# Two-layer encoder with expert-choice routing: top-k states in four quarters, and router weights that carry the norm's weights

## What is computed

```python
h = rms_norm(x, norm_ffn[i])
affinity = softmax(h @ w_router, axis=-1)          # 16 experts
gate, idx = lax.top_k(affinity.T, cap)             # cap = 2 * T / 16
xe = tokens[idx]
hid = silu(xe @ w_gate) * (xe @ w_up)
ye = (hid @ w_down) * gate[..., None]
out = zeros.at[idx].add(ye)
```

## Time and profile before

| | before |
|---|---|
| median of 3 runs | 1827.52 us |
| the profiled execution, its own time | 1825.45 us |
| span of the profile | 1823.6 us |
| PE busy | 1757.9 us (96%) |
| DVE busy | 1330.9 us (73%) |
| ACT busy | 1131.5 us (62%) |
| POOL busy | 234.7 us (13%) |
| mean DMA rate | 266 GB/s |

### The profile page before, as it was taken

One profiled execution on the slowest core, in us unless ns is written; L12 is line 12 of the kernel. 1 busy time (PEld: TensorE's weight loads), 2 busy tenths in 40 slices (PEclk: granted clock), 3 DMA queues, 4 the chain that ended last, 5 costly groups with the idle time before them and its releaser, 6 DMA issues.

```text
span 1823.6 us, 24589 instructions
## 1 busy us (share of the span) xinstructions
PE 1757.9 (96%) x10322; PEld 1386.7 (76%) x10322; DVE 1330.9 (73%) x1008; ACT 1131.5 (62%) x1185; POOL 234.7 (13%) x118
## 2 busy tenths in 40 slices
PE   6999989999999999999999999999999999999997
PEld 6888889977766776776779987997677677667765
DVE  4735455688888888888855556557888888888885
ACT  4343452457777777777743557335777777777774
POOL 0100000000110010010011100000112211311311
PEclk9999999999999999999999999999999999999998
DMA  4411123389999999999964012338999999999994
GB/s 161 102 45 56 43 69 107 156 321 396 396 375 388 393 379 382 394 382 377 396 200 104 21 39 55 106 118 326 376 394 383 378 390 393 377 383 390 375 393 141
DMA packets 155841, 486.00 MB, mean 266 GB/s; under 512 B 12199, under 2 KB 46119, under 8 KB 155687
## 3 DMA queue, kind: packets, MB, share of 16 engines
q1 hardware_dynamic: 148308, 459.26, 66.9%
q0 software_dynamic: 7424, 25.17, 5.9%
HBM read 454.26 MB, written 30.13 MB: 266 GB/s over the span
## 4 chain that ended last, share of the span: by engine, by line
PE 91%; DVE 3%; ACT 3%; issue 1%; DMA 1%; POOL 0%; POOLq 0%; SPq 0%; DVEq 0%; ACTq 0%
PE ps L1817 19%; PE ps L1819 19%; PE ps L1818 19%; PE ps L1515 5%; PE ps L1517 4%; PE ps L1516 4%; PE ps L1595 3%; PE ps L1469 3%; PE ps L1707 2%; PE ps L1709 2%; PE ps L1708 2%; PE ps L1567 2%; PE ps L1788 1%; PE ps L1584 1%; PE ps L1781 1%
## 5 line engine op out<-in xcount | busy, mean ns | idle before, releaser
L1320 DVE TENSOR_TENSOR w_lo<-ring,w_hi 128x2048 fp32r<-128x2048 f32 x384 | 876.7, 2291 | 144.5 <-ACT w_hi L1024 144.3
L1024 ACT ACTIVATE w_hi<-ring 128x2048 fp32r<-128x2048 f32 x384 | 735.6, 1917 | 275.0 <-PE ps L1819 268.2
L1817 PE MATMUL ps<-w_hi,xe_hi 128*96 128x512 f32 x1016 | 403.5, 397 | 0.0
L1819 PE MATMUL ps<-w_hi,xe_lo 128*96 128x512 f32 x1016 | 399.3, 393 | 0.0
L1818 PE MATMUL ps<-w_lo,xe_hi 128*96 128x512 f32 x1016 | 398.2, 392 | 0.0
L1819 PEld LDWEIGHTS ps<-w_hi,xe_lo 128*96 128x96 f32 x1016 | 163.9, 161 | 71.4
L1817 PEld LDWEIGHTS ps<-w_hi,xe_hi 128*96 128x96 f32 x1016 | 163.8, 161 | 69.8 <-DVE xe_lo L1419 5.9
L1818 PEld LDWEIGHTS ps<-w_lo,xe_hi 128*96 128x96 f32 x1016 | 164.3, 162 | 64.6
L1817 PE MATMUL ps<-w_hi,hid_hi 128*96 128x512 f32 x512 | 201.6, 394 | 0.0
L1819 PE MATMUL ps<-w_hi,hid_lo 128*96 128x512 f32 x512 | 201.1, 393 | 0.0
L1818 PE MATMUL ps<-w_lo,hid_hi 128*96 128x512 f32 x512 | 200.3, 391 | 0.0
(11 more groups left out here) (190 smaller groups left out, 2243.3 us busy)
## 6 DMA issues: line engine op xcount, KB each, us to landing
ring<-in_moe_w_gate SPq DMA_DIRECT2D x128, 1024.0 KB, 7.5
ring<-in_moe_w_up SPq DMA_DIRECT2D x128, 1024.0 KB, 8.9
ring<-in_moe_w_down SPq DMA_DIRECT2D x128, 1024.0 KB, 9.2
wbuf<-in_a_w_in SPq DMA_DIRECT2D x9, 1024.0 KB, 5.6
ffn_rows<-hrow SPq DMA_DIRECT2D x12, 512.0 KB, 2.7
wbuf<-in_b_w_in SPq DMA_DIRECT2D x5, 1024.0 KB, 7.8
unit_rows<-row SPq DMA_DIRECT2D x36, 132.0 KB, 1.8
bias<-bias_rows SPq DMA_DIRECT2D x4, 768.0 KB, 10.1
```

Of the source, the lines that this page charges most:

```text
L1024: nc.scalar.activation(w_hi[:, n % SPLIT], ring[:, n % RAW], ACT.Copy).then_inc(hi_split, 1)
L1320: nc.vector.tensor_tensor(w_lo[:, n % SPLIT], ring[:, n % RAW], w_hi[:, n % SPLIT].bitcast(F32), ALU.subtract).then_inc(lo_split, 1)
L1817: nc.tensor.matmul(out, hi[:, k, :], w_hi[:, n % SPLIT, i, cols], start=(k == 0), stop=False)
L1819: ins = nc.tensor.matmul(out, lo[:, k, :], w_hi[:, n % SPLIT, i, cols], start=False, stop=(k == KM - 1))
```

## The change

The norm's weights are multiplied into the router's weights (gain_router), so PE turns x itself for the router. hrow is made in one DVE instruction with both factors, one tile later (norm_row), and ACT scales it no more. The top-k states lie in four quarters of 32 partitions: each replacement (strike) reads one quarter and writes the next, so four successive states stand side by side, and one index search serves four rounds (find). The prompt's rows are rows 16 to 31 of the quarters; they join at round 6, and the rounds 8 and 9 are 256 columns wide. The results are packed by products with a constant mask (place) and brought to the layout of take by matmuls with a constant (expert). On SP, three pieces go ahead of the last row store, two behind it, and the sixth waits for the first gather. The idle products before the picks are 16 instead of 28. The two constants are loaded at the start, before the third weight chunk, and DVE waits for them with the other constants.

```diff
 C = CS + CP
-RAW, SPLIT = 6, 4
+RAW, SPLIT, FRONT = 6, 4, 3
 KP = 2
...
         buckets[BUCKETS, start + i] = MASKED
-    return {"c_buckets": buckets, "c_ident": np.eye(P, dtype=np.float32)}
+    row = np.arange(P)
+    quarter = np.zeros((P, 6, 8), np.float32)
+    for at, q in enumerate((0, 1, 2, 3, 2, 3)):
+        quarter[row // 32 == q, at, :] = 1.0
+    expert = (row[:, None] % 32 == np.arange(2 * NE)[None, :]).astype(np.float32)
+    return {"c_buckets": buckets, "c_ident": np.eye(P, dtype=np.float32), "c_quarter": quarter, "c_expert": expert}
...
 router = sb("router", [P, KM, NE])
+gain_col = sb("gain_col", [P, KM])
+quarter = sb("quarter", [P, 6, 8])
+expert = sb("expert", [P, 2 * NE])
+aff_p = sb("aff_p", [P, PT_, 2 * NE])
...
     hrow = sb("hrow", [P, NT, DM], scope=mo)
-    am = sb("am", [48, DEC_SEQ], scope=mo)
-    topi = sb("topi", [48, CS], U32, scope=mo)
-    pk_i = sb("pk_i", [48, P], scope=mo)
-    pk_g = sb("pk_g", [48, P], scope=mo)
+    am = sb("am", [P, DEC_SEQ], scope=mo)
+    top_v = sb("top_v", [P, 3, 8], scope=mo)
+    top_i = sb("top_i", [P, 3, 8], U32, scope=mo)
+    pick_i = sb("pick_i", [P, C], scope=mo)
+    pick_v = sb("pick_v", [P, C], scope=mo)
     xg = sb("xg", [C, 2, DM], scope=mo)
...
         sp.dma_start(router[:], d["moe_router"][layer].rearrange("(k p) e -> p k e", p=P)).then_inc(route_in, 16)
+        sp.dma_start(gain_col[:], bass.AP(d["norm_ffn"].tensor, layer * DM, [[1, P], [P, KM]]),
+                     allow_slow_non_contiguous=True).then_inc(route_in, 16)
...
             t = ORDER[i]
-            sp.wait_ge(row_scaled, NT * layer + i + 1)
+            sp.wait_ge(h_ready, NT * (2 * layer + 1) + i + 1)
             sp.dma_start(h_d[t * P:(t + 1) * P, :], hrow[:, t, :]).then_inc(h_out[i % 2], 16)
...
         sp.wait_ge(out_done, NT * (layer + 1))
-        for n in range(layer * LAYER_PIECES, layer * LAYER_PIECES + RAW):
+        first_piece = layer * LAYER_PIECES
+        for n in range(first_piece, first_piece + FRONT):
             load_piece(n)
         store_rows(NT - 1)
+        for n in range(first_piece + FRONT, first_piece + RAW - 1):
+            load_piece(n)
         sp.wait_ge(xg_in[0], 16 * (layer * NE // 2 + 1))
-        for n in range(layer * LAYER_PIECES + RAW, (layer + 1) * LAYER_PIECES):
+        for n in range(first_piece + RAW - 1, first_piece + LAYER_PIECES):
             load_piece(n)
-            if n == layer * LAYER_PIECES + RAW + 1:
+            if n == first_piece + RAW + 1:
                 store_sums(NT - 1)
...
-        def scale_rows(i):
-            t = ORDER[i]
-            act.wait_ge(rstd_ready, rstd_count(2 * layer + 1, i))
-            nc.scalar.activation(hrow[:, t, :], hrow[:, t, :], ACT.Copy, scale=rstd[:, t:t + 1]).then_inc(row_scaled, 1)
         def exp_route(part):
...
             act.wait_ge(rlog_ready, 2 * layer + part + 1)
+            act.wait_ge(rstd_ready, rstd_count(2 * layer + 1, (NT - PT_ if part == 0 else NT) - 1))
             for t in range(STREAM[part].start, STREAM[part].stop):
...
                 take_rows(i - 1)
-                scale_rows(i - 1)
             if i == NT - PT_:
...
         take_rows(NT - 1)
-        scale_rows(NT - 1)
         exp_route(1)
...
     nc.vector.memset(minus_half[:], -0.5)
+    nc.vector.memset(aff_p[:], 0.0)
     nc.vector.memset(rb, 1.0).then_inc(rb_set, 1)
...
-        def gain_row(i):
+        def norm_row(i):
             t = ORDER[i]
             dve.wait_ge(attn_added, NT * layer + i + 1)
-            nc.vector.tensor_tensor(hrow[:, t, :], x[:, t, :], gain[:], ALU.mult).then_inc(h_ready, 1)
+            dve.wait_ge(rstd_ready, rstd_count(2 * layer + 1, i))
+            nc.vector.scalar_tensor_tensor(hrow[:, t, :], x[:, t, :], rstd[:, t:t + 1], gain[:],
+                                           ALU.mult, ALU.mult).then_inc(h_ready, 1)
+        def gain_router():
+            dve.wait_ge(route_in, 32 * (layer + 1))
+            nc.vector.tensor_tensor(router[:], router[:], gain_col[:].unsqueeze(2).to_broadcast([P, KM, NE]),
+                                    ALU.mult).then_inc(router_ready, 1)
...
             step(nc.vector.reciprocal(lrec[:, ts], lsum[:, ts]), route_step)
-            nc.vector.tensor_tensor(aff[:, ts, :], lexp[:, ts, :],
+            nc.vector.tensor_tensor(aff[:, ts, :] if part == 0 else aff_p[:, :, NE:2 * NE], lexp[:, ts, :],
                                     lrec[:, ts].unsqueeze(2).to_broadcast([P, ts.stop - ts.start, NE]),
...
             else:
-                step(nc.vector.tensor_copy(am[32:32 + NE, 0:SEQ], ps[0:NE, 4, 0:SEQ]), route_step)
-        def top_round(rows, r, last):
-            cols, w = slice(8 * r, 8 * r + 8), DEC_SEQ if rows.start == 0 else SEQ
-            best = pk_g[rows, cols]
-            step(nc.vector.max(best, am[rows, 0:w]), route_step)
-            step(nc.vector.max_index(topi[rows, cols], best, am[rows, 0:w]), route_step)
-            if not last:
-                step(nc.vector.match_replace(am[rows, 0:w], best, am[rows, 0:w], -1.0), route_step)
-        SAMPLE, BOTH, PROMPT = slice(0, NE), slice(0, 48), slice(32, 32 + NE)
+                rows = am[quarter_of(JOIN), 0:SEQ]
+                step(nc.vector.tensor_tensor(rows, ps[0:2 * NE, 4, 0:SEQ], rows, ALU.add), route_step)
+        JOIN = 6
+        def quarter_of(r, count=2 * NE):
+            return slice(r % 4 * 32, r % 4 * 32 + count)
+        def largest(r):
+            rows = quarter_of(r, NE if r < JOIN else 2 * NE)
+            w = DEC_SEQ if r < CS // 8 else SEQ
+            step(nc.vector.max(top_v[rows, r // 4, :], am[rows, 0:w]), route_step)
+        def strike(r):
+            count = NE if r < JOIN else 2 * NE
+            w = DEC_SEQ if r + 1 < CS // 8 else SEQ
+            step(nc.vector.match_replace(am[quarter_of(r + 1, count), 0:w], top_v[quarter_of(r, count), r // 4, :],
+                                         am[quarter_of(r, count), 0:w], -1.0), route_step)
+        def find(group):
+            rows, w = (slice(0, P), DEC_SEQ) if group < 2 else (slice(0, 64), SEQ)
+            step(nc.vector.max_index(top_i[rows, group, :], top_v[rows, group, :], am[rows, 0:w]), route_step)
+        def place(group, src, dst):
+            at, n, rows = ((0, 4, P), (4 * 8, 6, P), (10 * 8, 2, 64))[group]
+            return nc.vector.tensor_tensor(dst[0:rows, at:at + 8 * n].rearrange("p (q j) -> p q j", j=8),
+                                           src[0:rows, group, :].unsqueeze(1).to_broadcast([rows, n, 8]),
+                                           quarter[0:rows, 0:n, :], ALU.mult)
...
         low_chunk(FIRST_OUT[layer] + 3)
+        gain_router()
         gains += 1
...
             if i == 1:
-                nc.vector.memset(pk_i[:], 0.0)
-                nc.vector.memset(pk_g[:], 0.0)
-                step(nc.vector.memset(am[:], -1.0), route_step)
+                nc.vector.memset(top_v[:], 0.0)
+                nc.vector.memset(pick_i[64:P, :], 0.0)
+                nc.vector.memset(pick_v[64:P, :], 0.0)
+                nc.vector.memset(am[:, SEQ:DEC_SEQ], -1.0)
+                step(nc.vector.memset(am[:, 0:SEQ], 0.0), route_step)
             if i == NT - PT_:
...
                 take_affinities(0)
-                for r in range(3):
-                    top_round(SAMPLE, r, False)
+                for r in range(4):
+                    largest(r)
+                    if r < 3:
+                        strike(r)
+                find(0)
+                strike(3)
             add_out(i)
-            gain_row(i)
+            if i >= 1:
+                norm_row(i - 1)
             row_means(2 * layer + 1, i)
-        top_round(SAMPLE, 3, False)
-        top_round(SAMPLE, 4, False)
+        largest(4)
+        norm_row(NT - 1)
+        strike(4)
+        largest(5)
+        strike(5)
         route_logits(1)
...
         take_affinities(1)
-        for r in range(5, CS // 8):
-            top_round(BOTH, r, False)
-        top_round(PROMPT, (CS - CP) // 8, True)
-        nc.vector.tensor_copy(pk_i[SAMPLE, 0:CS], topi[SAMPLE, :])
-        nc.vector.tensor_copy(pk_i[PROMPT, CS:C], topi[PROMPT, CS - CP:CS])
-        nc.vector.tensor_copy(pk_i[PROMPT, 0:CP], topi[PROMPT, CS - CP:CS])
-        nc.vector.tensor_copy(pk_g[PROMPT, CS:C], pk_g[PROMPT, CS - CP:CS]).then_inc(picks_ready, 1)
-        dve.wait_ge(picks_turned, layer + 1)
+        largest(6)
+        strike(6)
+        largest(7)
+        find(1)
+        strike(7)
+        largest(8)
+        strike(8)
+        largest(9)
+        find(2)
+        for group in range(3):
+            ins = place(group, top_i, pick_i)
+        ins.then_inc(picks_ready, 1)
+        for group in range(3):
+            ins = place(group, top_v, pick_v)
+        ins.then_inc(picks_ready, 1)
+        dve.wait_ge(picks_turned, 2 * layer + 1)
         nc.vector.tensor_scalar(take[0:CS, :], ps[0:CS, 5, 0:NE], float(SEQ), None, ALU.add)
```

(29 more changed lines are left out.)

6 lines of the change are left out of this document (4 added, 2 removed).

## The result

The changed kernel took 1829.12 us (median of 22 runs, 1825.79 to 1832.16). The kernel before took 1825.94 us in the same job (22 runs, 1823.00 to 1829.37). The ratio is 1.0014, with a 95% interval from 1.0009 to 1.0020: some 2.6 us slower, where 4.7 us less was forecast. The time lies outside the range given.

A forecast was written before the change was run, and what follows sets the result against it. The prediction took the DVE chain plus the idle products on PE to bound the stage before the expert loop, with the gather next. 2 layers x 2.35 = 4.7 us off 1827.52 gave 1822.8 us, range 1821.0 to 1826.0.

The forecast's parts named there:

- The DVE chain: DVE's top-k work up to the packing, in each layer: shorter by 0.29 and then 2.39 us.
- the stretch up to the logits: DVE from the first MAX8 to the second part's logits: 4.26 us instead of 4.55, a gain of 0.29.
- the joined rounds: DVE's top-k rounds after the prompt's rows join: 5.45 us instead of 7.84, a gain of 2.39.
- rival 3: Quarter-shifting replacements and finds over 128 rows take two passes on DVE: +3.5 us a layer, 1834.5 us; chance 0.05.
- The gain of 2.35 a layer: Stage from output projection to expert loop: idle products start at 369.65 instead of 372.02; between 1.9 and 2.5 us.
- Ring pieces and the gather: SP and POOL, layer 0: pieces from 357.0, last store lands 370.0, gather starts 370.9 and lands after 4.7 us.
- 2.3 us to spare: Layer 0: gather lands at 375.6, idle products end at 377.9; a gather of 7 us would use it up.
- rival 2: The gather, delayed by pieces 3 and 4 to 9.5 us, becomes the bound: 1827.5, half of it 1825; chance 0.1.
- Lateness in the loop at zero: Layer 0's expert loop: a ring piece comes 1 to 2 us late, some 4 us is hidden, so no cost.
- The clock left at one layer in two: PE's gap before the picks grows from 2.66 to 2.95 us; half clock still in one layer, 1.33 us either side.
- Rival 1: The longer gap before the picks halves PE's clock in both layers: gain 3.4 us, 1824.1 us; chance 0.2.
- The sum: Whole kernel: 2 layers x 2.35 = 4.7 us less, 1822.8 us for the median.

The follow-up runs named there:

- e14: Changed kernel with row 4's stores behind three ring pieces, 27 idle products before the picks, last sum's store and next gain's load 12 pieces later: 1821.55 us.
- e11: Kernel before the change with 39 instead of 28 idle products ahead of the picks: 1823.82 us, ratio 0.9991.
- e5: Changed kernel with 27 instead of 16 idle products ahead of the picks: 1827.94 us, ratio 1.0005.
- e12: Changed kernel with row 4's stores behind the first three ring pieces and 27 idle products ahead of the picks: 1822.11 us, ratio 0.9979.
- e1: Changed kernel with norm_row(i - 1) ahead of add_out(i) instead of behind it: 1825.62 us, ratio 1.0000.
- e4: Changed kernel with the last sum's store and the next gain's load 12 pieces later on SP: 1826.25 us, ratio 0.9995.
- e7: Changed kernel's new top-k and packing alone, with norm, row scaling and row store order as in the kernel before: 1825.04 us, ratio 0.9997.
- e8: Kernel before with norm_row, gain_router and the changed SP order; its own top-k and 28 idle products kept: 1828.90 us, ratio 1.0023.
- e6: Changed kernel with norm_row(i - 1) ahead of add_out(i) and 27 idle products ahead of the picks: 1823.58 us, ratio 0.9986.
- e9: Changed kernel with norm_row(i - 1) ahead of add_out(i), 27 idle products ahead of the picks and 26 instead of 36 behind: 1824.13 us.
- e15: Changed kernel, row 4's stores behind three pieces, 27 idle products before picks, six pieces ahead of gather, sum store and gain load 12 later: 1824.42 us.
- e10: Changed kernel with row 4's stores behind three ring pieces, 27 idle products ahead of the picks and 26 behind them: 1823.94 us, ratio 0.9993.
- e13: Changed kernel with row 4's stores behind three ring pieces, 27 idle products before the picks, all six pieces ahead of the gather: 1824.47 us.
- e3: Changed kernel with ring pieces 3 and 4 behind the first gather on SP: 1837.48 us, ratio 1.0054.

## Why the prediction was wrong, point by point

- **The DVE chain: right to 0.3.** Forecast 2.7 up to the packing, measured 2.4: the stretch up to the logits gained 0.15 instead of 0.29 (one of its waits is the 0.17 for POOL), and the joined rounds took 5.60 instead of 5.45. No second pass for shifted or full-height forms: rival 3 falls. The idle products were to start at 369.65; on before's clock they start at 369.8. Between e14 and e11, both at full clock, the turning is 2.16 us earlier in layer 0 (2.10 + 0.06, where e11 stands as before) and 2.16 in layer 1 (3.62 against 1.46 from add_out(5) on). The gain of 2.35 a layer was there, as 2.2.
- **Ring pieces and the gather: the starts right, two sizes off.** Pieces were to start near 357.0, measured 357.35 on before's clock. The last store was to land at 370.0, it landed at 371.6; the gather was to start at 370.9, it started at 372.5. And it took 7.3 us where I took 4.7. The text named the limit itself, 2.3 us to spare, or 7 us; with 1.6 us of it gone ahead of the gather, it came 0.23 us after the idle products, which the half clock had lengthened by 1.6. At full clock PE waits 1.74 (e5). So rival 2 was real in kind, with 7.3 instead of its 9.5, and the half clock hid it. I took 4.7 from a row in which no ring piece issued ahead of the gather was still on its way. Here two were, the last with 6.7 us to go (last section).
- **Lateness in the loop at zero: the step that failed.** I reckoned 1 to 2 us late and let some 4 us of it be hidden, since ACT may split a piece three ahead of PE. Measured: 2.52 us of PE's time, and 1.7 more as the clock fell once more behind it. The lateness was larger than I reckoned: I had the piece 1 us earlier than before, and it landed 2.7 later on before's clock (403.14 - 1.0 against 399.43), since the gather in front of it, forecast 4 us earlier, wasn't earlier at all. But the 1 to 2 us that I had reckoned stall PE too: in e12 the piece lands where it did before, PE is 1.9 earlier, and 1.60 are lost. The cover wasn't there because DVE's order is fixed: xe_lo of the next expert stands behind the low part of the late piece, and PE needs xe_lo when it starts the piece before that one. That is one piece (2.8 us) and xe_lo's own 0.95 sooner than the products on the late piece, nearly all of my 4 us. The kernel before had 0.06 us to spare there (404.68 against 404.74). The row of 0.16 us was the sign of it; I had read it as "thin" and not as the bound.
- **The clock left at one layer in two: failed.** The gap was reckoned right (2.95), its effect not. Rival 1 was the case, at twice its price: 1.6 and 2.7 us for the two layers against 0 and 1.33 before, 3.0 us in all, where I gave 1.3. That is from one profile of each kernel. The rule of the Trainium skill (TensorE: Matmul & The Clock Gate, Part 1) that I had set against the change, that the watch on the array's activity runs free of the kernel, pointed the right way.
- **The sum.** 2 x 2.2 = 4.3 gained; 3.0 lost to the clock before the picks, 4.1 in layer 0's loop. With 0.2 for the gather that is 3.0 slower; the ratio says 2.6. The two profiles are 6.5 apart, of which 1.0 at the start and 1.7 at the start of layer 1 are no part of it. The remaining 3.8 are 0.8 above the sum: the two stages are 0.6 shorter in the profiles where these terms make 1.1, and the rest is in small steps that I did not trace.

## What to carry to other kernels

When a stage gets shorter, ask of each load behind it whether it gets earlier by the same amount; if not, what the stage gains can be lost at the first instruction that stands behind that load in an engine's fixed order. Reckon the cover up to that instruction; a slot count ("three pieces ahead") doesn't give it. Cover that hides a wait (idle products) has to be sized again with the stage, at both ends: a gap in front of it cost 1.6 to 2.7 us here on top of its own length. And where two orders of one queue are possible, move what nobody waits for (here 1 MB of sums and gains) behind what somebody does, before touching the order of the rest.

## What was not expected of the hardware

- **What follows a gap.** A gap of 2.95 us before the picks was followed by the lower clock (0.50, 1.2 GHz) in 11 of 12 profiled layers (the changed kernel, e1 to e4, e7). Gaps of 2.66 and 2.67 gave 2 of 4 (before, e8), and gaps of 0.21 to 0.50 none of 18 (e5, e6, e9 to e15). Where PE waits for add_out(5), 2.00 us gave 3 of 6 (e1, e6, e9) and the usual 1.39 none of 28. So longer gaps did it more often, but 2 of 4 against 11 of 12 are too few to show that the step from 2.66 to 2.95 matters. Nor did a gap's length alone decide: of the eight waits for the first gather of 0.65 us and more, each with a wait of 0.90 for xe_hi soon behind it, five were followed by the lower clock, those of 0.65 (e15) and 0.72 (e10) among them, and those of 0.91 (e13), 1.27 (e9) and 1.65 (e15) were not. The 72 passes took 8.28 to 8.31 us at full clock and 9.6 to 11.1 with a fall in them.
- **The gather beside ring loads.** What counts is how long the ring pieces issued ahead of it still take when it starts. In the first gathers of all these kernels, both layers: none or up to 3.5 us left, 4.2 to 4.7 us (but 5.3 once in e7 and 5.7 and 5.8 in e3 with none left, which I can't explain); 3.9 to 5.7 left, 5.3 to 6.6; 6.1 and 6.7 left, 6.9 and 7.3; 7.9 to 8.7 left, 8.2 to 9.3. So with 3.9 us or more left, a gather landed between 0.5 us ahead of those pieces and 2.2 behind them, and not 4.5 behind. The Trainium skill (DMA: Bandwidth & Descriptors, Queues, rings and completion order) says that each engine takes turns between the queues that have work for it; that fits a gather that moves beside the pieces.
- **Rows cost nothing in a search.** FIND_INDEX8 over 128 rows takes 0.70 us for 512 columns, over 16 rows 0.67.
